# First expert table: three routing tiles at half pace, gate matrices from unit 64 on

## The reference

```
q  = h @ w_pq                       # 8 heads, two halves of 128
s1 = q[:, :, 0] . sub_keys1         # 128 scores per head and half
s2 = q[:, :, 1] . sub_keys2
v1, i1 = top_k(s1, 16); v2, i2 = top_k(s2, 16)
top_s, sel = top_k(v1 + v2 (all pairs), 16);  eidx = i1 * 128 + i2 at sel
gate = softmax(top_s)
act  = gelu(sum_d u_tab[eidx] * h)
out  = sum_k gate * act * v_tab[eidx];   x = x + out
```

## Time and profile before

| | us |
|---|---|
| median of 3 runs (3904.06 to 3905.03) | 3904.68 |
| the profiled execution | 3904.86 |
| its span, first to last instruction | 3903.1 |
| Gelu of unit 0, Gelu of unit 127 (start, from the span's start) | 1442.92, 2770.25 |
| TensorE busy | 3586.4 (92%) |
| VectorE busy | 2555.1 (65%) |
| ScalarE busy | 1290.1 (33%) |
| GpSimd busy | 878.6 (23%) |

### The profile page before, as it was taken

One profiled execution on the slowest core, in us unless ns is written; L12 is line 12 of the kernel. 1 busy time (PEld: TensorE's weight loads), 2 busy tenths in 40 slices (PEclk: granted clock), 3 DMA queues, 4 the chain that ended last, 5 costly groups with the idle time before them and its releaser, 6 DMA issues. The chain is left out here.

```text
span 3903.1 us, 50109 instructions
## 1 busy us (share of the span) xinstructions
PE 3586.4 (92%) x19479; PEld 3335.9 (85%) x19479; DVE 2555.1 (65%) x3620; ACT 1290.1 (33%) x1610; POOL 878.6 (23%) x609
## 2 busy tenths in 40 slices
PE   8999997885998989987999899898799999999995
PEld 6888886664886879987999899898799999999995
DVE  4111112885224138999777677676698989898996
ACT  5221122332214223332555455554222222222222
POOL 0000000000000000121223233233255545454451
PEclk9999998777998989998999999999899999999998
DMA  5222222534415234555899889889899898989896
GB/s 203 102 97 107 110 99 58 189 127 159 149 69 205 81 137 147 216 214 209 334 344 348 335 334 364 323 333 343 323 357 368 353 373 352 376 346 378 350 355 226
DMA packets 186998, 965.63 MB, mean 247 GB/s; under 512 B 18657, under 2 KB 61345, under 8 KB 86098
## 3 DMA queue, kind: packets, MB, share of 16 engines
q1 hardware_dynamic: 108082, 506.07, 34.6%
q0 software_dynamic: 61264, 426.27, 28.0%
q10 hardware_dynamic: 17488, 31.06, 2.2%
HBM read 865.77 MB, written 97.55 MB: 247 GB/s over the span
## 5 line engine op out<-in xcount | busy, mean ns | idle before, releaser
L1513 DVE TENSOR_TENSOR units_wlo<-units_raw,units_whi 128x2048 fp32r<-128x2048 f32 x256 | 586.2, 2290 | 335.8 <-ACT units_whi L1509 334.3
L1509 ACT CAST units_whi<-units_raw 128x2048 fp32r<-128x2048 f32 x256 | 491.8, 1922 | 864.4 <-PE outputs_vp L2200 624.1
L1725 PE MATMUL hidden_hp<-dense_hi,units_whi 128*128 128x384 f32 x2048 | 709.9, 347 | 41.5 <-DVE units_wlo L1513 41.5
L1726 PE MATMUL hidden_hp<-dense_lo,units_whi 128*128 128x384 f32 x2048 | 697.6, 341 | 0.0
L1727 PE MATMUL hidden_hp<-dense_hi,units_wlo 128*128 128x384 f32 x2048 | 695.9, 340 | 0.0
L2198 PE MATMUL outputs_vp<-outputs_w_hi,units_whi 128*128 128x384 f32 x2032 | 678.9, 334 | 0.4 <-DVE units_wlo L1513 0.4
L2200 PE MATMUL outputs_vp<-outputs_w_hi,units_wlo 128*128 128x384 f32 x2032 | 678.7, 334 | 0.0
L2199 PE MATMUL outputs_vp<-outputs_w_lo,units_whi 128*128 128x384 f32 x2032 | 678.7, 334 | 0.0
L1667 POOL DMA_INDIRECT hidden_row<-u_rows,expert_ids x192 | 323.4, 1684 | 1193.4 <-DVE dots L1948 809.9
L2135 DVE SCALAR_TENSOR_TENSOR accg<-outputs_row,outputs_w_op,accg 128x2048 f32<-128x2048 f32 x190 | 445.9, 2347 | 50.7 <-DMA outputs_row<-v_rows,outputs_id 48.1
L2002 POOL DMA_INDIRECT outputs_row<-v_rows,outputs_id x192 | 318.7, 1660 | 527.3 <-DVE accg L2135 471.5
(11 more groups left out here) (351 smaller groups left out, 4688.1 us busy)
## 6 DMA issues: line engine op xcount, KB each, us to landing
units_raw<-u_units SPq DMA_DIRECT2D x128, 1024.0 KB, 6.3
units_raw<-v_units SPq DMA_DIRECT2D x128, 1024.0 KB, 7.2
in_proj_raw<-w_in SPq DMA_DIRECT2D x48, 1024.0 KB, 5.6
hidden<-hidden_hid SPq DMA_DIRECT2D x128, 192.0 KB, 2.8
gate_mat<-units_big SPq DMA_DIRECT2D x12, 2048.0 KB, 22.5
units_big<-hidden SPq DMA_DIRECT2D x16, 1536.0 KB, 10.0
units_big<-gate_mat SPq DMA_DIRECT2D x16, 1536.0 KB, 15.7
out_proj_raw<-w_out SPq DMA_DIRECT2D x16, 1024.0 KB, 7.2
```

Of the source, the lines that this page charges most:

```text
L1509: self.nc.scalar.copy(self.hi[s][:], self.raw[s][:]).then_inc(self.hi_done, 1)
L1513: self.nc.vector.tensor_tensor(self.lo[s][:], self.raw[s][:], self.hi[s][:].bitcast(F32), ALU.subtract).then_inc(self.lo_done, 1)
L1725: mm(o, un.hi[s][:, x, :], h_hi[:, x, :], start=x == 0, stop=False)
L1726: mm(o, un.hi[s][:, x, :], h_lo[:, x, :], start=False, stop=False)
```

## The change

Tiles 0 and 1 are routed as before, in units 0 to 15. Tiles 2, 3 and 4 take a step in every second unit, so that routing goes on until unit 62 and not 39. 70 gathers and not 22 are done until the gate matrices begin; that begins at unit 64 and not 40, and the 96 groups are spread over 57 units and not 81.

```diff
-    first_gate, after_gates = 8 * TILES, NKEYS - 7
+    starts, steps = [0, 8, 16, 32, 48], [1, 1, 2, 2, 2]
+    first_gate, after_gates = 64, NKEYS - 7
...
-        spread = [(0, 0), (17, 0), (first_gate, 22), (NKEYS, NGATHER)]
+        spread = [(0, 0), (17, 0), (first_gate, 70), (NKEYS, NGATHER)]
...
+    def step_at(n):
+
+        for t in range(TILES):
+            if starts[t] <= n < starts[t] + 8 * steps[t] and (n - starts[t]) % steps[t] == 0:
+                return t, (n - starts[t]) // steps[t]
+        return None, None
...
-                if n % 8 == 0 and n // 8 + 1 < TILES:
-                    load_q(n // 8 + 1)
+                t, j = step_at(n)
+                if j == 0 and t + 1 < TILES:
+                    load_q(t + 1)
...
-                s, t, j = n % 2, n // 8, n % 8
+                s, (t, j) = n % 2, step_at(n)
...
-                if t + 1 < TILES:
+                if t is not None and t + 1 < TILES:
                     (turn if j < 4 else score)(t + 1, j % 4)
-                if j == 2 and 2 <= t - 1 < TILES - 1:
+                if j == 2 and t > 2:
                     turn_back(t - 1)
                 if n == first_gate - 1:
                     turn_back(TILES - 1)
...
-                if n < first_gate:
-                    route(n // 8, n % 8)
+                t, j = step_at(n)
+                if t is not None:
+                    route(t, j)
```

More of the change, by code:

```diff
@@ L1799, in _ @@
                 nc.scalar.activation(act_out[s][:], bank[s][:, 0:ND], ACT.Gelu).then_inc(gelus, 1)
-                if t + 1 < TILES:
+                if t is not None and t + 1 < TILES:
                     (copy_q if j < 4 else copy_s)(t + 1, j % 4)
-                if j == 2 and 2 <= t - 1 < TILES - 1:
+                if j == 2 and t > 2:
                     keep(t - 1)
-                if t < TILES and j == 7:
+                if j == 7:
                     act.wait_ge(exps_in, t + 1)
```

## The result

| | kernel before | changed kernel |
|---|---|---|
| median of the first timing, us | 3904.37 | 3832.97 |
| ratio, 95% interval | | 0.9818 (0.9806 to 0.9830) |
| median of a second timing, us | 3903.64 | 3832.76 |
| ratio, 95% interval | | 0.9817 (0.9804 to 0.9829) |
| span of the profiled execution, us | 3903.1 | 3827.0 |

What follows compares the result with a forecast made beforehand. TensorE's work sets a floor of 1020.1 us for units 17 to 127; VectorE bounds routing, and stores delay loads. Gains of 14 (routing), 16.3 (turn back) and 28 (stores) sum to 58: 3847 us, range 3829 to 3877.

Steps and rivals of the forecast that it cites:

- The account of the kernel before: Units 17 to 127: 155.5 us lost over a floor of 1020.1: routing 38.1, turn to gate matrices 16.3, stores 101.0.
- Routing at half pace: Routing steps in every second unit, until unit 62: loss 24 us instead of 38.1, gain 14.
- The last turn back: TensorE's turn back behind unit 63: softmax done in time, the 13.87 us wait and slow unit go, gain 16.3 us.
- Denser groups: Gate matrices, two groups in 39 of 57 units: double units last 10.1 us on TensorE, no new bound, no cost.
- The signs named: Gelu of unit 63 near 2021 us, of 127 near 2712; low-part waits within 3; nine store waits of 3 to 5.
- The stores: Twelve 2 MB stores ahead of unit loads: nine lose 6.4 us, two 1.0, the last 13.4; 73.0 not 101.0, gain 28.
- The step from none to one double unit: Loss per store fell from 9.4 to 7.9 us; the same step again was taken for two double units, 6.4.
- The rival of stores as dear as before: DMA traffic sets the waits behind stores, so 101 us stay: gain 30, 3875 us; chance 0.2.
- The slower rival: Stores 47 us apart leave the queue no time to empty, each costs 13.4 us: 3935 us; chance 0.04.
- The rival in which all waits get shorter: Stores' losses fall to 45 us in sum: gain 86, 3819 us, halfway 3833; chance 0.1.
- Rows late in the routing stretch: Rows or loads late in routing, 23 pairs of units each waiting 1.5 us: 35 us lost, 3882 us; chance 0.08.

Runs made afterwards that it cites:

- The second profile: The changed kernel as it is, run once more beside the kernel before: 0.9817 (0.9804 to 0.9829) of it.
- turn: The kernel before with the gate matrices beginning at unit 41 and not 40: 0.9959 of the kernel before, 0.9966 when timed more often.
- gates64: The kernel before with gate matrices from unit 64 and not 40, routing pace and gathers' places kept: 0.9851, then 0.9855 of the kernel before.
- gathers: The changed kernel with the old table of gathers, 22 until unit 40 and 68 until 64: 3849.87 us, 0.9857 of the kernel before.
- onegather: The kernel before with 104 gathers until unit 40, then one per unit and not two: 4000.73 us.
- double: The changed kernel with gate matrices from unit 73 and not 64, two groups in each of 48 units: 3818.74 us, 0.9784 of the kernel before.
- the parts: The changed kernel with each 2 MB store cut into four of 512 KB, one behind each of four units' loads: 3800.07 us, 0.9731 of the kernel before.

## Why the prediction was right, and where not

*The account of the kernel before* held: three places, and nothing else moved. Each of the 77 us lies in one of them, and the floor of 8.32, 0.89 and 0.45 us gives the undisturbed units of every kernel here.

*Routing at half pace* was forecast at a loss of 24 and measured at 26.5 in the profile of the first run. The waits for the low part were put at 19 and are 14.9, the wait for queries at 2.7 and is 4.3, the longest at 3 and is 3.1; the clock was put at 3 and took 7.2. These errors cancel in part, so that the sum is nearer than its terms. The second profile has 29.3 lost. That VectorE is the bound is shown by the old table of gathers.

*The last turn back* was forecast at a gain of 16.3 and has it, since the softmax is done in time. As a term by itself it was too large: moved alone it brings 6.5 us at its place. The other 10 were VectorE's lag, which stays at unit 40 wherever routing keeps the old pace (turn, gates64) and is gone with the half pace; 4.7 us stand at unit 62 instead.

*Denser groups* cost nothing, as forecast: undisturbed double units take 10.1 us.

*The signs named* came: Gelu of unit 63 at 2023 (2021 was named), longest wait for the low part 3.1, no slow unit 64, waits before the gate matrices of 4.8 us at most (eight, where nine were named), stores at units 75 and 118 without a loss. The Gelu of unit 127 is at 2693.5 where 2712 was named, and that is the next step.

*The stores* are the step that was mis-sized: 28 us of gain were forecast, 49.6 measured, so 73 us left against 51.4. The nine stores put at 6.4 each lose 37.2 in sum, 4.1 each (eight at 4.6, the one of unit 84 nothing). The two named as cheap lose nothing where 1.0 each was put, the last one 14.3 where 13.4 was put. The step from none to one double unit, 1.5 us, was too small. It is the difference of two means, and the mean with one double unit held a store that landed late, the one of unit 116 (its landing, and the window of its two late units, 11.4 lost):

```profile
DMA to landing us min/median/max: 24.0/24.0/24.0
```

```profile
2657.80:2687.70 29.90, 20.11 (x115) 19.82 (x115) 16.02 (x21) 10.40 (x17) 8.04 (x4) 0.83 0.76 291
```

The profiles show what slack is worth at like landings. These are the stores (the last of a kernel left out) that landed in 21.6 to 22.9 us in seven profiles: the kernel before, turn (two), gates64 (two), gathers, and the changed kernel's second. The loss is that of units n + 1 to n + 3 for a store of unit n:

| double units ahead | stores | mean landing, us | mean loss, us |
|---|---|---|---|
| none | 10 | 22.4 | 9.3 |
| one | 14 | 22.1 | 6.7 |
| two | 11 | 22.1 | 4.6 |

So a double unit takes some 2.4 us off the loss and not 1.5, and slack alone brings a store from 9.3 to 4.6. Sooner landings are the smaller part, which the forecast left out: longer units also thin the gathers. With two double units, 20 stores that landed in 17.1 to 20.4 us lose 3.0 in the mean. Over the first eleven stores the mean landing is 21.9 us in the kernel before, 19.7 in the changed kernel's second profile and 19.6 in both of gates64. That a quick landing alone is enough is shown by onegather. The rival of stores as dear as before is refuted by every profile with groups from 64 on. The slower rival too: double has them still closer and is faster. The rival in which all waits get shorter, with 3833 at its halfway point, had the right size of the whole; I gave it 0.1, though it differed from the forecast only in this term. That the time lies in the stated range rests on the range having taken in half of this rival.

*Rows late in the routing stretch* did not come: it moved 317 GB/s, no dot product waited for its rows, and the one transfer that TensorE waited for is the queries'.

The Trainium skill, DMA: Bandwidth & Descriptors, Queues, rings and completion order, has the DMA engines take turns between rings that have work, and one ring's transfers start in order. The landings of 11.7, 14.1 and 22.5 us with no, one and two gathers per unit agree with the first half, and the gain of the parts with the second.

What puts a store among the quickest shows over all profiles with landings and two gathers in most units: eleven stores stand right behind a unit with a single gather. Ten of them landed in 14.3 to 15.9 us and lost at most 1.1; one, in the kernel with the old table of gathers, took 21.7 and lost 4.5. No other store of 2 MB there landed in under 16.8. Open is what spreads the others from 16.8 to 29.4 us, and why two profiles of one kernel differ by 18 us in what the stores cost.

## What to carry to other kernels

Where a large transfer and the loads that an engine lives on share one queue, cut the large one and deal it out behind several loads: that brought another 33 us on top of the 71 of the change, and the traffic stayed the same. Before a wait's length is booked as a gain, look at which other engine is behind at that moment; move the wait alone to see what was under it. When work per iteration changes, count anew every stream that is paced by the iteration, since a slower pace also thins what competes with the transfer. And before a step between two means is carried on to a third case, look whether one odd row made it.

## What the runs showed of the hardware

The same 2 MB store from the stage buffer to memory, in 1 KB pieces, lands in 11.7 us with unit loads alone beside it, in 14.1 with one gather of 128 rows per unit, and in 22.0 to 22.8 with two, all medians of a kernel. Where two of three units have two groups and so last longer, the medians with two gathers are 19.5 to 21.1. I had not expected the step from one to two to be so much larger than the first.
